# Expert weights of a mixture-of-experts layer: three whole transfers with 8 KB rows in place of six halves

## The reference

```
def expert_block(args):
    xb, e = args
    hid = jax.nn.silu(xb @ w_eg[e]) * (xb @ w_eu[e])
    return hid @ w_ed[e]
```

## Time and profile before

| | us |
|---|---|
| median of 3 runs (lowest, highest) | 1129.3 (1128.2, 1130.95) |
| the profiled execution | 1128.56 |
| its span | 1126.7 |

### The profile page before, as it was taken

How to read it: one execution, slowest core, us unless ns; L and a number is a source line. 1 busy time by engine, 2 the same in 40 slices (tenths; PEclk the granted TensorE clock), 3 DMA queues, 4 the chain that set the end, 5 groups by cost and what they waited for, 6 DMA issues and landing times.

```text
span 1126.7 us, 16009 instructions
## 1 busy us (share of the span) xinstructions
PE 1081.3 (96%) x5521; PEld 894.9 (79%) x5521; DVE 707.3 (63%) x924; ACT 561.3 (50%) x739; POOL 377.8 (34%) x270
## 2 busy tenths in 40 slices
PE   4999999999999999999999999979999999999997
PEld 3888888878888888888888888767888888877862
DVE  6767887873076521222222655579999999988855
ACT  6447776762264100000003322258888888877843
POOL 2313222215223223233230000125666666654520
PEclk9999999999999999999999999989999999999999
DMA  9100000113003121221203352579999999999829
GB/s 269 30 7 9 7 11 9 39 38 88 25 1 103 39 56 38 56 56 39 58 5 106 138 169 93 206 252 388 385 385 374 372 353 360 341 358 360 332 105 370
DMA packets 108856, 181.07 MB, mean 161 GB/s; under 512 B 32384, under 2 KB 69760, under 8 KB 108800
## 3 DMA queue, kind: packets, MB, share of 16 engines
q1 hardware_dynamic: 98432, 163.51, 42.1%
q0 software_dynamic: 10368, 16.80, 4.0%
HBM read 174.50 MB, written 26.74 MB: 179 GB/s over the span
## 4 chain that ended last, share of the span: by engine, by line
PE 74%; SPq 9%; DVE 6%; DMA 5%; issue 3%; ACT 3%; POOLq 0%; ACTq 0%; DVEq 0%
PE ps L405 21%; PE ps L407 20%; PE ps L406 20%; SPq L542 7%; PE ps L782 3%; PE ps L744 2%; DMA raw_e<-in_w_exp_up_dram 2%; PE ps L1026 2%; SPq L538 1%; DMA yin<-y_dram 1%; DVE negm L1599 1%; DMA xre<-in_x_dram 1%; DVE pt_lo L1632 1%; DVE we_lo L1942 1%; PE ps L955 1%
## 5 line engine op out<-in xcount | busy, mean ns | idle before, releaser
L1942 DVE TENSOR_TENSOR we_lo<-raw_e,we_hi 128x2048 fp32r<-128x2048 f32 x105 | 240.0, 2287 | 33.9 <-ACT we_hi L1394 33.5
L1394 ACT ACTIVATE we_hi<-raw_e 128x2048 fp32r<-128x2048 f32 x105 | 200.5, 1911 | 15.2 <-DMA raw_e<-in_w_exp_up_dram 8.8
L405 PE MATMUL ps<-ht_hi,w_hi 128*128 128x512 f32 x416 | 163.2, 392 | 0.3 <-ACT u_t L1292 0.3
L407 PE MATMUL ps<-ht_hi,w_lo 128*128 128x512 f32 x416 | 162.0, 390 | 0.0
L406 PE MATMUL ps<-ht_lo,w_hi 128*128 128x512 f32 x416 | 162.0, 389 | 0.0
L399 POOL CAST w_hi<-raw 128x1024 fp32r<-128x1024 f32 x34 | 36.6, 1077 | 276.9 <-PE ps L407 209.1
L1766 DVE TENSOR_TENSOR mix<-ps,mix 128x512 f32<-128x512 f32 x16 | 11.1, 691 | 173.6 <-PE ps L407 173.6
L405 PE MATMUL ps<-we_hi,xst_hi 128*128 128x512 f32 x280 | 115.8, 414 | 0.4 <-DVE xst_lo L1946 0.4
L407 PE MATMUL ps<-we_hi,xst_lo 128*128 128x512 f32 x280 | 110.3, 394 | 0.0
L406 PE MATMUL ps<-we_lo,xst_hi 128*128 128x512 f32 x280 | 109.2, 390 | 0.0
L407 PEld LDWEIGHTS ps<-ht_hi,w_lo 128*128 128x128 f32 x416 | 78.1, 188 | 16.5
(11 more groups left out here) (329 smaller groups left out, 2494.7 us busy)
## 6 DMA issues: line engine op xcount, KB each, us to landing
raw_e<-in_w_exp_gate_dram SPq DMA_DIRECT2D x70, 512.0 KB, 6.6
raw_e<-in_w_exp_up_dram SPq DMA_DIRECT2D x70, 512.0 KB, 16.5
raw_e<-in_w_exp_down_dram SPq DMA_DIRECT2D x70, 512.0 KB, 8.7
raw<-in_w_in_dram SPq DMA_DIRECT2D x27, 512.0 KB, 3.9
yin<-y_dram SPq DMA_DIRECT2D x16, 512.0 KB, 9.6
xin<-in_x_dram SPq DMA_DIRECT2D x8, 512.0 KB, 8.2
xre<-in_x_dram SPq DMA_DIRECT2D x8, 512.0 KB, 5.8
h_dram<-h SPq DMA_DIRECT2D x8, 512.0 KB, 3.1
```

Of the source, the lines that this page charges most:

```text
L405: pe.matmul(dst, st[0], mv[0], start=first, stop=False)
L407: return pe.matmul(dst, st[1], mv[0], start=False, stop=last)
L1394: act.activation(we_hi[c % 4][:, :], raw_e[c % NS][:, :], ACT.Copy).then_inc(sem("w_hi_ready"), 1)
L1942: dve.tensor_tensor(we_lo[c % NS][:, :], raw_e[c % NS][:, :], we_hi[c % 4][:, :].bitcast(F32), ALU.subtract).then_inc(sem("w_lo_ready"), 1)
```

## The change

All three matrices of an expert are fetched whole, each in one DMA of 1 MB with rows of 8 KB. Gate and up lie in the two buffers that held g=0 and g=1 before; the pieces of the splits and products stay the same, but the g=0 and g=1 pieces are read (and their low parts written) in two runs of 4 KB, one in each of the two buffers. For this the buffers are ordered so that the pair lies within one of two ranges, and a pair's distance is a multiple of 4 KB. The first split of a pair waits for both DMAs, the second for neither. As the pair is in use until the g=1 product, the load into the g=0 buffer waits for one more product. The down load of expert 0 goes into the first batch and the g=0 load of expert 1 into the second, and SP's wait for the stored rows moves ahead of two loads.

```diff
-        slots = (8, 16, 24, 172, 180, 188, 196, 92, 100, 116, 124, 164)
+        slots = (8, 16, 172, 180, 24, 188, 196, 92, 116, 124, 164, 100)
+        ring = [at("ring", 8, [P, 25, D], F32), at("ring_far", 116, [P, 22, D], F32)]
+        ring_lo = [at("ring_lo", 8, [P, 25, D], F32R), at("ring_lo_far", 116, [P, 22, D], F32R)]
...
+        def landed(it, c):
+            name, base = slot_full(c)
+            return sem(name), it * 16 + (base + 16 * (c // NS + 1))
+        def side_by_side(it, j):
+            return sorted((piece(0, it, j)[0] % NS, piece(1, it, j)[0] % NS), key=lambda i: slots[i])
+        def gate_up(parts, g, it, j):
+            far = int(j % 4 != 0)
+            lo, hi = ((slots[i] - (8, 116)[far]) // 4 for i in side_by_side(it, j))
+            return parts[far][:, lo + g:hi + g + 1:hi - lo, :]
... load
-                    wait(sp, "group_used", n - (NS - 1))
-                    for i in range(2):
-                        w_d, h = (wd_d, i) if g == 2 else ((wg_d, wu_d)[i], g)
-                        sp.dma_start(raw_e[c % NS][:, i * D:(i + 1) * D], w_d[bass.ds(src, 1)].rearrange("e p n -> (e p) n")[:, h * D:(h + 1) * D]).then_inc(
-                            sem(slot_full(c)[0]), 16)
+                    wait(sp, "group_used", n - (NS - 1 - (g == 0 or last or g == 1 and j % 4 == 0)))
+                    if g == 2:
+                        w_d, dst = wd_d, raw_e[c % NS][:, :]
+                    else:
+                        w_d = (wg_d, wu_d)[side_by_side(it, j).index(c % NS)]
+                        far = int(j % 4 != 0)
+                        u = (slots[c % NS] - (8, 116)[far]) // 4
+                        dst = ring[far][:, u:u + 2, :].rearrange("p a n -> p (a n)")
+                    sp.dma_start(dst, w_d[bass.ds(src, 1)].rearrange("e p n -> (e p) n")).then_inc(
+                        sem(slot_full(c)[0]), 16)
... the first loads
                         load(0, 0, 0)
                         load(1, 0, 0)
-                        load(0, 0, 1)
+                        load(2, 0, 0)
                     if t == NT - 2:
                         sp.wait_ge(sem("mt_lo_ready"), NT)
+                        load(0, 0, 1)
                         load(1, 0, 1)
-                        load(2, 0, 0)
... SP, expert
                         sp.wait_ge(sem("xs_full1"), 16)
+                        for i in range(2):
+                            sp.wait_ge(sem(f"h2_stored{i}"), 16 * NT // 2)
                     if left(2) and not fetched:
                         load(1, it, j + 2)
                     if left(1) and not fetched:
                         load(2, it, j + 1, not left(2))
-                    if isinstance(it, int) and it == 0 and j == 1:
-                        for i in range(2):
-                            sp.wait_ge(sem(f"h2_stored{i}"), 16 * NT // 2)
... TensorE, columns
-                    wh, wl = (w[:, :].rearrange("p (a k f) -> p a k f", a=2, f=DE) for w in (we_hi[c % 4], we_lo[c % NS]))
+                    wh = we_hi[c % 4][:, :].rearrange("p (a k f) -> p a k f", a=2, f=DE)
+                    wl = gate_up(ring_lo, g, it, j)
...
-                                 (wh[:, :, i, :], wl[:, :, i, :]), k == 0, k == KD - 1)
+                                 (wh[:, :, i, :], wl[:, :, i * DE:(i + 1) * DE]), k == 0, k == KD - 1)
... ACT, high
-                    name, base = slot_full(c)
-                    act.wait_ge(sem(name), it * 32 + (base + 32 * (c // NS + 1)))
+                    if g == 2:
+                        act.wait_ge(*landed(it, c))
+                        wait(act, "group_used", n - 3)
+                        act.activation(we_hi[c % 4][:, :], raw_e[c % NS][:, :], ACT.Copy).then_inc(sem("w_hi_ready"), 1)
+                        return
+                    if g == 0:
+                        act.wait_ge(*landed(it, c))
+                        act.wait_ge(*landed(it, piece(1, it, j)[0]))
                     wait(act, "group_used", n - 3)
-                    act.activation(we_hi[c % 4][:, :], raw_e[c % NS][:, :], ACT.Copy).then_inc(sem("w_hi_ready"), 1)
+                    act.activation(we_hi[c % 4][:, :].rearrange("p (a n) -> p a n", a=2), gate_up(ring, g, it, j),
+                                   ACT.Copy).then_inc(sem("w_hi_ready"), 1)
... DVE, low: for g of 0 and 1
+                    dve.tensor_tensor(gate_up(ring_lo, g, it, j), gate_up(ring, g, it, j),
+                                      we_hi[c % 4][:, :].rearrange("p (a n) -> p a n", a=2).bitcast(F32),
+                                      ALU.subtract).then_inc(sem("w_lo_ready"), 1)
```

More of the change, by code:

```diff
@@ L1941, in low @@
                     dve.wait_ge(sem("w_hi_ready"), n + 1)
-                    dve.tensor_tensor(we_lo[c % NS][:, :], raw_e[c % NS][:, :], we_hi[c % 4][:, :].bitcast(F32), ALU.subtract).then_inc(sem("w_lo_ready"), 1)
+                    if g == 2:
+                        dve.tensor_tensor(we_lo[c % NS][:, :], raw_e[c % NS][:, :], we_hi[c % 4][:, :].bitcast(F32), ALU.subtract).then_inc(sem("w_lo_ready"), 1)
+                        return
+                    dve.tensor_tensor(gate_up(ring_lo, g, it, j), gate_up(ring, g, it, j),
+                                      we_hi[c % 4][:, :].rearrange("p (a n) -> p a n", a=2).bitcast(F32),
+                                      ALU.subtract).then_inc(sem("w_lo_ready"), 1)
                 def rows_low(it, j):
```

## The result

The changed kernel takes 1133.24 us (median of 6 runs, 1132.09 to 1136.37), the kernel before beside it 1128.64; the ratio is 1.0046 with a 95% interval of 1.0033 to 1.0059. The change makes the kernel slower by 0.46%, 3.7 to 6.7 us by the interval. The forecast was 1126.2 us with a range to 1132.5: the sign is wrong and the time lies 0.7 us outside. The profiled executions stand at 1132.09 us, span 1130.2, against 1128.56 and 1126.7: 3.5 us.

The account below looks back on a forecast made before the run. TensorE was taken to bound the expert stage, except 5.7 us lost near its end to a few late DMA engines; 2.5 + 0.2 - 5.4 - 0.4 = -3.1 took the median from 1129.3 to 1126.2 us, range 1122.8 to 1132.5.

Parts of the forecast that it names:

- The g=0 load is issued one product later: Expert stage, weight loads: issue 3.0 us later, hidden by the last engines' queue; taken +0.2 us, ends 0 and +3.0.
- Rival C: Start of expert stage: last engines run dry, later issue counts in full, long rows' gain lost; +5.1, 1134.4 us; chance 0.15.
- its two signs: Rival C's signs in the expert stage: period longer before 994 us, and landings under 9 us at 800.
- Rows of 8 KB: Expert weight loads: fewer row starts and completions save 0.2 us an expert over 27 experts; -5.4 us, ends 0 and -7.0.
- the fixed part of 7: Weight loads: fixed cost per row start, taken as 7 ns, ends 0 and 10; 24 starts saved per engine and expert.
- the 6 ns for a completion: Weight loads: each DMA completion costs an engine about 6 ns; 3 fewer on each engine and expert.
- The first split waits for both: ACT's first split of an expert waits for both whole matrices, the second landing 2.5 us later; +2.5, ends 0 and 3.4.
- Two-buffer reads, moved steps: Splits and products reading two buffers, and the moved store waits and loads on SP: each forecast at 0.
- Issues before the stage: Before the expert stage: fewer weight issues ahead of the x rows, only row starts saved; -0.4 us, ends 0 and -2.7.
- the prediction's estimate: DMA rows: a separate estimate by the Trainium skill's cycles, said to come to the same size as rival D, 1129.2 us.

Follow-up runs that it names:

- the 4 KB form: The changed kernel with each matrix fetched by two DMAs with 4 KB rows, same buffers, waits and order: 1136.88 us, 1.0073 against the kernel before.
- the run with both edits: The kernel before with the first split waiting for both loads and every g=0 load issued one product later, rows still 4 KB: 1136.24 us, 1.0065.

## Why the prediction was wrong, step by step

The failed step is *"The g=0 load is issued one product later"*, "taken +0.2". Alone it measures +3.0 (its upper end), and beside the pair wait +4.6 in single profiled executions (spans: 1133.6 with both, 1129.0 with the pair wait alone). The prediction argued that the last engines have "their queue of 10.8 us at that point", so nothing runs dry. That is the median of a window from 780 to 820 us. At its first loads the lag is not built up yet: the earlier trace rows give 9.0 us for 740 to 780, and the two up halves issued at 783.04 and 786.02, from which the step itself reads its 3.0 us, had their last counts 7.7 and 9.3 us later. The step's mechanism, a queue that never runs dry, is what failed: between 764 and 792 us the engines' busy share fell three times, once to a tenth. Rival C had put the limit at 9.6 us, named the place, "the first experts up to about 800 us", and the time, 1134.4; the measured 1133.24 is nearest to it. It got 0.15, though a row met its condition. Its near hit in time is part luck: it had the long rows win nothing, and of its two signs only one came (the period is longer before 994 us; the landings of the issues from 795 to 805 us are 11.3 to 14.1 us, not under 9). Lead lost at the start didn't come back where every g=0 load was issued late (+2.8 at the last count); where only the first ones were, most of it did.

*Rows of 8 KB*: -5.4 was forecast, 3.0 to 3.8 measured against the 4 KB form. The trace's single packets last 159 ns with 4 KB and 309 with 8 KB (medians), so two short ones lose 9 ns: the fixed part of 7 was nearly right for their length. No run shows the 6 ns for a completion; the packets of 4 bytes in the traces last 9 ns (median), and the term would change by 0.01 us an expert. From the down matrix of expert 6 to the last one, the last counts take 275.8 us before (800.0 to 1075.8) and 271.5 after (803.1 to 1074.6), 0.16 us an expert in the mean in place of 0.2. But the gain isn't even, as the step had it: 3.1 us of it are won from expert 6 to 12, and from there to expert 33 both kernels take 212.3 us. Why is open.

*The first split waits for both*: +2.5 forecast, +2.4 (1.0 to 3.7) measured alone, 3.2 in the chain of the changed kernel. Right, in mechanism and size.

*Two-buffer reads, moved steps*: 0 forecast. The splits' durations are as before, and the run with both edits differs from the one with 4 KB rows by less than the times can tell.

*Issues before the stage*: -0.4 forecast. The first transposes shown start at 778.81 in place of 778.61: nothing of it is to be seen.

The sum was 2.5 + 0.2 - 5.4 - 0.4 = -3.1. By the runs it is 6.9 for the two order edits together and -3.4 for the rest (1133.6 and 1130.2), +3.5 in the profiled spans. If the two edits together cost more than their sum, as the profiled executions have it, no step of the prediction knew of it.

What bounds the stage was read rightly, the few last engines included: evening out their load brought back the 5.7 us in the stage that the prediction had counted as lost (4.8 in the time of the kernel).

## What to carry to other kernels

Ask of a load that is issued later what the queue holds at each of its issues, the first ones above all; a median over a window in which a lag builds up hides the start. Here, lead lost there was kept to the end when every such load stayed late, mostly won back when only the first were, and cost nothing where no engine lagged. Where a few DMA engines are late, first look at which partitions the sparse transfers touch: a new order of rows won 0.46% here, while longer rows, bought with a coarser order, lost 0.46%. A gain at one resource can be outweighed when the same edit makes consumers wait for twice the data.

## What the runs showed of the hardware that was not expected

- Rows of 8 KB move 2.8% more than two of 4 KB from 820 to 1050 us (85.42 and 83.08 MB, same order of work), in one profiled execution of each; the kernel before with the down matrix alone whole moved 85.17 where it had moved 83.45, so the figure is no measure of the long rows' share. The 3 cycles a packet of the Trainium skill ("DMA: Bandwidth & Descriptors", Why small descriptors are slow) had stood for 1.1% in the prediction's estimate; the measured 2.8% is nearer to the 2.7% (0.2 of 7.5 us) that the prediction took from the rows, and so is the packets' own length: two of 159 ns against one of 309, 2.8%.
- Where the real rows of gathers and scatters lie among the partitions sets the time: 0.9954 (0.9939 to 0.9969) by the order of the rows alone, and 88.19 MB in place of 83.45 from 820 to 1050 us.
- DMA engines that run dry for a few us (9.46 MB in place of 10.84 from 764 to 792 us) cost nothing with the rows spread (0.9957), and 3.0 us with the rows packed (9.44 MB, 1.0031).
- A gain of 2.9 us at the end of one stage was gone after the next in the one profiled execution, with a granted clock of 0.71 and 0.81 in two stretches there.
